# Five K-tile pairs in place of four by seven products in the two output stages of a two-layer float32 block

## The reference, cut to what matters

```
gate, up = split(h @ w_ffn_in)            # 2048 -> 2 x 5632
x = x + rms_norm((silu(gate) * up) @ w_ffn_out, g)   # first block; 5632 -> 2048
h = h + (silu(a) * b) @ ffn_w_out                    # second block, then a last rms_norm
```

## Time and profile before

| | us |
|---|---|
| median of 3 runs (lowest, highest) | 2390.25 (2389.15, 2392.04) |
| the profiled execution: its own time | 2391.39 |
| the profiled execution: its span | 2389.4 |
| TensorE busy in the span | 2369.1 (99%), 12027 instructions |
| VectorE busy | 1848.3 (77%), 2570 instructions |
| ScalarE busy | 1398.8 (59%), 1939 instructions |
| fo1, from its first unit to its last four | 1037.01 to 1262.57 |
| fo2, the same | 2147.10 to 2371.03 |

### The profile page before, as it was taken

How to read it: one execution, slowest core, us unless ns; L and a number is a source line. 1 busy time by engine, 2 the same in 40 slices (tenths; PEclk the granted TensorE clock), 3 DMA queues, 4 the chain that set the end, 5 groups by cost and what they waited for, 6 DMA issues and landing times.

```text
span 2389.4 us, 34793 instructions
## 1 busy us (share of the span) xinstructions
PE 2369.1 (99%) x12027; PEld 1977.8 (83%) x12027; DVE 1848.3 (77%) x2570; ACT 1398.8 (59%) x1939; POOL 195.2 (8%) x252
## 2 busy tenths in 40 slices
PE   9999999999999999999999999999999999999998
PEld 7888888887888888888887888998888888888887
DVE  5568878677899999987667535767799999997766
ACT  5665458656666666655445445655666666664444
POOL 1000000000111111200000000000121111111000
PEclk9999999999999999999999999999999999999999
DMA  7775554555889787866566775344788887867655
GB/s 233 244 217 177 165 152 165 167 186 176 273 205 248 207 230 227 222 199 208 196 212 196 219 231 168 126 140 133 241 229 243 212 246 207 234 176 242 217 179 176
DMA packets 249217, 485.23 MB, mean 203 GB/s; under 512 B 19770, under 2 KB 22074, under 8 KB 248592
## 3 DMA queue, kind: packets, MB, share of 16 engines
q1 hardware_dynamic: 216768, 410.51, 52.5%
q0 software_dynamic: 31760, 72.16, 14.9%
q10 hardware_dynamic: 576, 1.05, 0.1%
HBM read 474.21 MB, written 9.44 MB: 202 GB/s over the span
## 4 chain that ended last, share of the span: by engine, by line
PE 94%; DVE 3%; DMA 2%; ACT 1%; issue 1%; SPq 0%; ACTq 0%; DVEq 0%
PE g L1466 10%; PE g L1467 10%; PE g L1468 10%; PE g L362 6%; PE g L364 6%; PE g L363 6%; PE g L1973 4%; PE g L1975 4%; PE g L1974 4%; PE m L1294 3%; PE m L1295 3%; PE m L1293 3%; PE g L1294 2%; PE g L1295 2%; PE g L1293 2%; DMA raw<-in_w_ffn_out 1%
## 5 line engine op out<-in xcount | busy, mean ns | idle before, releaser
L350 DVE TENSOR_TENSOR wl<-raw,wh 128x1024 fp32r<-128x1024 f32 (+1 forms) x500 | 601.0, 1216 | 328.5 <-ACT wh L346 321.7
L346 ACT ACTIVATE wh<-raw 128x1024 fp32r<-128x1024 f32 (+1 forms) x499 | 519.1, 1052 | 468.1 <-PE g L364 128.8
L1466 PE MATMUL g<-wh,act_hi 128*128 128x512 f32 x640 | 250.5, 391 | 0.0
L1468 PE MATMUL g<-wh,act_lo 128*128 128x512 f32 x640 | 249.3, 390 | 0.0
L1467 PE MATMUL g<-wl,act_hi 128*128 128x512 f32 x640 | 249.3, 389 | 0.0
L1232 ACT ACTIVATE wh<-in_x 128x1024 fp32r<-128x1024 f32 (+1 forms) x160 | 152.7, 955 | 106.6 <-PE g L1468 69.5
L1466 PE MATMUL g<-wh,ht_hi 128*128 128x512 f32 x544 | 212.1, 390 | 0.3 <-DVE wl L350 0.3
L1467 PE MATMUL g<-wl,ht_hi 128*128 128x512 f32 x544 | 211.8, 389 | 0.0
L1468 PE MATMUL g<-wh,ht_lo 128*128 128x512 f32 x544 | 211.8, 389 | 0.0
L1394 DVE TENSOR_TENSOR wl<-raw,wh 128x1024 fp32r<-128x1024 f32 x160 | 195.5, 1222 | 13.1 <-ACT wh L1389 3.4
L362 PE MATMUL g<-wh,act_hi 128*128 128x512 f32 x512 | 203.3, 397 | 0.9 <-DVE wl L350 0.4
(11 more groups left out here) (546 smaller groups left out, 5116.8 us busy)
## 6 DMA issues: line engine op xcount, KB each, us to landing
raw<-in_w_in SPq DMA_DIRECT2D x111, 512.0 KB, 4.5
raw<-in_w_ffn_in SPq DMA_DIRECT2D x106, 512.0 KB, 4.8
raw<-in_ffn_w_in SPq DMA_DIRECT2D x106, 512.0 KB, 4.8
raw<-in_w_ffn_out SPq DMA_DIRECT2D x88, 512.0 KB, 5.3
raw<-in_ffn_w_out SPq DMA_DIRECT2D x88, 512.0 KB, 5.2
raw<-in_nsa_w_in SPq DMA_DIRECT2D x80, 512.0 KB, 4.3
raw<-in_w_out SPq DMA_DIRECT2D x32, 512.0 KB, 4.3
raw<-in_nsa_w_out SPq DMA_DIRECT2D x32, 512.0 KB, 4.9
```

What stands on the lines that cost most here:

```text
L346: nc.scalar.activation(wh[:, j % SLOTS, 0:n], raw[:, j % SLOTS, 0:n], ACT.Copy).then_inc(hi_done, 1)
L350: nc.vector.tensor_tensor(wl[:, j % SLOTS, 0:n], raw[:, j % SLOTS, 0:n], wh[:, j % SLOTS, 0:n].bitcast(F32), ALU.subtract).then_inc(lo_don ...
L1466: nc.tensor.matmul(dst, h, whk, start=(t in starts and k == 0), stop=False)
L1468: ins = nc.tensor.matmul(dst, l, whk, start=False, stop=(last and k == 1))
```

## The change: five pairs, new order, three rounds of sums

`FO_K` goes from 4 to 5. The order is written anew: blocks begin at positions 9, 18, 26, 35, 43 and 60, 69, 78, 87, 96 of 108. Sums of x come in three rounds, at positions 5, 14 and 28, the third for one pair alone. The first of the four sums now takes the place of the second row tile of the even K-tile in `ht_hi` and `ht_lo`, which blocks don't read, by an instruction of its own on ScalarE and VectorE; the other three stay in the buffers `fo_hi` and `fo_lo`, laid out anew.

```diff
-FO_K = 4
-FO_GAPS = ((10, 0), (5, 0), (1, 4), (1, 6), (1, 8)), ((6, 0), (6, 0), (4, 3), (1, 6), (1, 9))
-FO_SUMS_AT = (6, 15)
+FO_K = 5
+FO_GAPS = (((9, 0), (5, 0), (2, 2), (0, 5), (0, 4), (1, 6)),
+           ((6, 0), (5, 0), (5, 0), (0, 5), (0, 5), (1, 7)))
+FO_SUMS_AT = (5, 14, 28)
+FO_ROUNDS = (FO_K + 1) // 2
...
-        SUMMED = 3 * 2 + 2 + 3 * (FO_K // 2)
+        SUMMED = 3 * 2 + 2 + 3 * FO_ROUNDS
...
+        def in_round(r):
+            return min(2, FO_K - 2 * r)
...
                 if n - 2 in FO_SUMS_AT:
-                    b = FO_SUMS_AT.index(n - 2) + 1
-                    act_sums_hi(act, fo_sums[:, :, :, :], fo_hi[:, 2 * (b - 1):2 * b, :, :], summed_no(name, b) + 1)
+                    r = FO_SUMS_AT.index(n - 2)
+                    act.wait_ge(ff_summed, summed_no(name, r + 1) + 1)
+                    w = in_round(r)
+                    nc.scalar.activation(first_sums(ht_hi, 4 * r, w), fo_sums[:, 0:w, 0, :], ACT.Copy)
+                    act_sums_hi(act, fo_sums[:, 0:w, 1:4, :], fo_hi[r][:, :, :, :], summed_no(name, r + 1) + 1)
...
                 if n in FO_SUMS_AT:
-                    dve_sums_of_x(dve, ht_hi, ht_lo, 4 * FO_SUMS_AT.index(n), fo_whole, fo_sums)
+                    dve_sums_of_x(dve, ht_hi, ht_lo, 4 * FO_SUMS_AT.index(n), fo_whole, fo_sums, in_round(FO_SUMS_AT.index(n)))
                 if n - 2 in FO_SUMS_AT:
-                    b = FO_SUMS_AT.index(n - 2) + 1
-                    k = slice(2 * (b - 1), 2 * b)
-                    dve_sums_lo(dve, fo_sums[:, :, :, :], fo_hi[:, k, :, :], fo_lo[:, k, :, :], summed_no(name, b) + 1)
-                    dve.wait_ge(ff_summed, summed_no(name, b + 1))
+                    r = FO_SUMS_AT.index(n - 2)
+                    dve.wait_ge(ff_summed, summed_no(name, r + 1) + 2)
+                    w = in_round(r)
+                    nc.vector.tensor_tensor(first_sums(ht_lo, 4 * r, w), fo_sums[:, 0:w, 0, :], first_sums(ht_hi, 4 * r, w).bitcast(F32), ALU.subtract)
+                    dve_sums_lo(dve, fo_sums[:, 0:w, 1:4, :], fo_hi[r][:, :, :, :], fo_lo[r][:, :, :, :], summed_no(name, r + 1) + 1)
+                    dve.wait_ge(ff_summed, summed_no(name, r + 2))
```

More of the change, by code:

```diff
@@ L168, in build @@
         fo_sums = at("fo_sums", [P, 2, 4, P], o_al + 4096)
-        fo_hi = at("fo_hi", [P, FO_K, 4, P], o_ah, F32R)
-        fo_lo = at("fo_lo", [P, FO_K, 4, P], o_ah + 8192, F32R)
+        fo_hi = [at(f"fo_hi{r}", [P, 2 - r // 2, 3, P], o_ah + (0, 3072, 12288)[r], F32R) for r in range(FO_ROUNDS)]
+        fo_lo = [at(f"fo_lo{r}", [P, 2 - r // 2, 3, P], o_ah + (6144, 9216, 13824)[r], F32R) for r in range(FO_ROUNDS)]
         fo_kept = {"fo1": at("fo_kept1", [P, T, NB], o_ga + 4096), "fo2": at("fo_kept2", [P, T, NB], o_gb)}
@@ L1181, in pe_seven, with dve_sums_of_x @@
             product(3, 1, of_x(1, 1), g[:, 1, :], False, False).then_inc(unit_used, 1)
-        def dve_sums_of_x(dve, hi, lo, k0, whole, sums):
-            tiles = [b[:, k0:k0 + 4, :].bitcast(F32).rearrange("p (s k) (t n) -> p s k t n", s=2, t=T) for b in (hi, lo)]
+        def dve_sums_of_x(dve, hi, lo, k0, whole, sums, pairs=2):
+            tiles = [b[:, k0:k0 + 2 * pairs, :].bitcast(F32).rearrange("p (s k) (t n) -> p s k t n", s=pairs, t=T) for b in (hi, lo)]
+            whole, sums = whole[:, 0:pairs], sums[:, 0:pairs]
             link_d(dve, nc.vector.tensor_tensor(whole[:, :, :, :, :], tiles[0], tiles[1], ALU.add))
@@ L1200, in dve_sums_lo, with first_sums, fo_block_sums @@
             nc.vector.tensor_tensor(lo, sums, hi.bitcast(F32), ALU.subtract).then_inc(ff_summed, 1)
-        def first_sums(buf, r):
-            k0 = 2 * SEVEN_K + 4 * r
-            return buf[:, k0:k0 + 4:2, P:2 * P]
+        def first_sums(buf, k0, pairs=2):
+            return buf[:, k0:k0 + 2 * pairs:2, P:2 * P]
+        def in_round(r):
+            return min(2, FO_K - 2 * r)
+        def fo_block_sums(name, b):
+            return lambda n: ((fo_hi[b // 2][:, b % 2, n - 1, :], fo_lo[b // 2][:, b % 2, n - 1, :]) if n else
+                              (ht_hi[:, 2 * b, P:2 * P], ht_lo[:, 2 * b, P:2 * P]))
         def block_sums(b):
@@ L1510, in pe_out @@
                         pe.wait_ge(ff_summed, summed_no(name, 2 + b // 2))
-                    pe_seven(pe, cyc, n, ht_hi, ht_lo, 2 * b, lambda k: (fo_hi[:, b, k, :], fo_lo[:, b, k, :]),
+                    pe_seven(pe, cyc, n, ht_hi, ht_lo, 2 * b, fo_block_sums(name, b),
                              b == 0, b == FO_K - 1, s["pair0"][1] + c + 1)
@@ L1675, in opening @@
                 for r in range(2):
-                    ins = nc.scalar.activation(first_sums(act_hi, r), sums[r][:, :, 0, :], ACT.Copy)
+                    ins = nc.scalar.activation(first_sums(act_hi, 2 * SEVEN_K + 4 * r), sums[r][:, :, 0, :], ACT.Copy)
                 ins.then_inc(ff_summed, 1)
@@ L1718, in opening @@
                 for r in range(2):
-                    ins = nc.vector.tensor_tensor(first_sums(act_lo, r), sums[r][:, :, 0, :], first_sums(act_hi, r).bitcast(F32), ALU.subtract)
+                    ins = nc.vector.tensor_tensor(first_sums(act_lo, 2 * SEVEN_K + 4 * r), sums[r][:, :, 0, :], first_sums(act_hi, 2 * SEVEN_K + 4 * r).bitcast(F32), ALU.subtract)
                 ins.then_inc(ff_summed, 1)
```

## The result

The changed kernel takes 2396.9 us (median of 8 runs, 2394.33 to 2400.65) against 2390.28 (2389.15 to 2392.04) for the kernel before: ratio 1.0026, 95% interval 1.0017 to 1.0035. The forecast was 2391.7 with a range of 2388.0 to 2395.5. The sign was right, the time lies above the range, and the runs spread over 6.3 us where those of before spread over 2.9.

A forecast was written before the change was run, and what follows sets the result against it. TensorE, busy 99% of the span, was taken as the bound. The terms -2.72 + 1.4 + 0.9 + 0 + 0 + 1.93 = +1.5 us on the median 2390.25 gave 2391.7 us, with an 8-in-10 range of 2388.0 to 2395.5.

The forecast's parts named there:

- What bounds the kernel: Whole kernel: TensorE is busy 99% of the span, so only fewer products or TensorE waiting can move the time.
- Products: Output stages fo1 and fo2: 12 products fewer at 0.2267 us each, 2.72 us less on TensorE.
- the gain stands: Rival, chance 0.19: third round and fo2's close fit, -2.72, or -3.3 with the third block's wait gone: 2387.0 us.
- The third round: Third block of each output stage: VectorE's 1.9 us sums of x make TensorE wait 1.4 us in fo1, 0.9 in fo2.
- Second passes: Second pass of each output stage: five blocks start from a full ring of loaded weight slots; taken as 0.
- The end of fo1: Close of fo1: copying out the third column chunk comes a unit later; taken as 0, upper end 1.93 us.
- The end of fo2: Last four units of fo2: VectorE's closing steps delay their lo's, 1.93 us on the path, ends 0.8 and 3.0.
- The opening of fo1: Start of fo1: one wait grows about 0.3 us, the third block's goes; together 0, ends -1.6 and +1.4.
- the ring of loads becomes the bound: Rival, chance 0.14: two loads a step, one us longer, no longer fit in the first passes; 2396.6 us.
- From the profile to the median: Whole kernel: the profiled execution lies 1.14 us above the median, so 2392.9 us profiled became a forecast of 2391.7.

The follow-up runs named there:

- f1: The changed kernel with plain units' loads in both output stages bringing only 512 of 1024 columns: 2387.47 us, ratio 0.9986 against the kernel before.
- f2: The changed kernel with each block's three sums of weights in the output stages made for half their columns: 2391.34 us.
- h1: e3 plus a second own slot for the first weights of every other block, loaded inside the block before: 2390.0 us.
- e3: The changed kernel with the third round at position 32, not 28, and ten units, not eight, behind the last block of pass two: 2392.69 us.
- h2: e3 with the eight returning pieces of x issued two by two at the start of pass one's first four blocks: 2391.15 us.
- h4: The second slot of h1 and moved x of h2, with four blocks a pass and the kernel before's gaps and rounds: 2389.89 us.
- h3: e3 with both the second slot of h1 and the moved pieces of x of h2: 2387.81 us, ratio 0.9987 against the kernel before.
- f3: The changed kernel with the third round at 32 and pass two respaced: four units, two gaps of six, two of five: 2394.77 us.

## Why the prediction was wrong, step by step

**What bounds the kernel** was right, and so was the view that only TensorE's waits could take the gain away.

**Products**: right. TensorE has 12015 instructions, and f1, in which no output stage waits, is 3.5 us under the kernel before: the rival "the gain stands" put 3.3 on products and the third block's wait together.

**The third round**: right in place and size. It took 1.87 us (1099.70 to 1101.57; 1.9 forecast) between the lo's of the third and fourth quarter:

```profile
1098.57 1.22 DVE L352 TENSOR_TENSOR wl<-raw,wh 128x1024 fp32r<-128x1024 f32 x1
1099.70 0.69 DVE L1189 TENSOR_TENSOR fo_whole<-ht_hi,ht_lo 128x512 f32<-128x512 f32 x1
...
1101.28 0.29 DVE L1195 TENSOR_TENSOR fo_sums<-fo_whole,fo_sums 128x128 f32<-128x128 f32 x1
1101.49 2.35 DVE L352 TENSOR_TENSOR wl<-raw,wh 128x1024 fp32r<-128x1024 f32 x2
```

The third quarter lasted 2.44 us in place of 1.36 in fo1 and 2.43 in fo2: 1.08 and 1.07 against 1.4 and 0.9. The estimate by the Trainium skill (VectorE: DVE Perf Modes, The TRN2 errata) was 1.85.

**Second passes: this step failed.** "Five blocks five units apart start from a full ring; a step loses 0.7 or gains 0.2 by the intervals above. I take 0." In the profiled run TensorE waits at no block of a second pass, so the 0 itself came out there; what failed is the full ring that it rests on, and that the end of fo1 was to find. The steps of fo1 lost 2.5, 0.7, 0.2 and 0.7 of lead, and 4.28 us were gone at the fifth block. In fo2 the first step alone lost 3.8, and the others lay between 0.5 lost and 0.3 won. So the intervals were about right for a ring that is already low; that the first step takes most of a full ring's lead I left out. Two ends of opposite sign were averaged to 0, although the trace of before showed where the round comes from: the same two loads and sums in series. What that round hides was left out too: all loads wait while the sums are made, then come in one burst. f1, f2 and h1 show it by taking away bytes, sums and one load of the burst: 9.4, 5.6 and (against e3) 2.7 us.

**The end of fo1, taken as 0**, followed from it and paid 1.81, the largest miss of the sum inside the trace (its upper end was 1.93). VectorE's rows there, of the changed kernel, show the last two lo's of the last four starting only at 1266.10, behind the closing steps:

```profile
1258.79 0.68 DVE L1557 TENSOR_TENSOR fo_step<-fo_kept,m 128x512 f32<-128x512 f32 x1
1259.39 1.22 DVE L352 TENSOR_TENSOR wl<-raw,wh 128x1024 fp32r<-128x1024 f32 x1
1260.53 0.68 DVE L1561 TENSOR_TENSOR fo_kept<-fo_step,m 128x512 f32<-128x512 f32 x1
1261.24 1.23 DVE L1571 TENSOR_TENSOR g<-g,fo_kept 128x1024 f32<-128x1024 f32 x1
1262.51 1.23 DVE L352 TENSOR_TENSOR wl<-raw,wh 128x1024 fp32r<-128x1024 f32 x1
...
1264.96 1.22 DVE L513 TENSOR_TENSOR y_a<-g,g_b 128x1024 f32<-128x1024 f32 x1
1266.10 2.35 DVE L352 TENSOR_TENSOR wl<-raw,wh 128x1024 fp32r<-128x1024 f32 x2
```

**The end of fo2**: the size was right (1.93 forecast, 2.2 measured), the reason only in half. I laid VectorE's old rows under the new order, as if place alone decided. f1 has that place and no wait: with a full ring the lo's run far enough ahead to let the closing steps pass between (in fo2 the last lo, behind all of them, begins 2.35 us after TensorE began the last four units there, at 2370.15 against 2367.80, and 4.50 in the changed kernel, at 2377.91 against 2373.41).

**The opening of fo1**: taken as 0 net, about +1 measured (fo1 lost 0.86 + 1.36 - 1.08 = 1.1 us beyond the third round up to its last four units, most of it up to the third block's start). h2 gives it to the pieces of x.

**The rival "the ring of loads becomes the bound"** had 0.14 and 2396.6 us, 0.3 from the result. That the number came so near is luck: it priced 11.2 us of late loads in the first passes, less 6.3 of cover, and the trace has 1.5 us of idle at their units and blocks beside the third round's, nearly all in fo1. Its mechanism was the right one, its place only in half: I put it in the first passes, by the pieces of x (h2: 1.5 us), and gave the second passes nothing. What counted against it there, a full ring in the earlier trace rows, was read at the first block of the pass, before the denser blocks had drawn on it.

**From the profile to the median**: I carried the old distance over (1.14 above the median). The distance turned to 1.2 below: 2.3 of the 5.1 us by which the forecast missed. An explanation, not shown, is that a drained ring passes each late load on to TensorE. For it speaks the spread of f1 (1.6 us with half the bytes), and h4 (1.4), h3 (3.5) and e3 (5.6) fit; f3 (3.4, with an empty ring), h1 (6.4, with a fuller one) and h2 (6.1) don't. Why loads land later in some executions stays open.

## What to carry to other kernels

A full ring at the start of a stretch is a stock, not an income: work out what one round of it takes (loads as they land in their burst, and every step in series with them) against what the consumer needs. Do so for the first round by itself, since a full ring waits for its consumer: here that round left 1.75 and 0.50 of 4.28 us, and the later rounds gave nothing back. A piece on a side engine that seems to stand in the wrong place may cost nothing with the ring full, as in f1, so first ask why it was empty. By the times, a load moved into a pause of the DMA engines was worth more here than the new order of the same burst, and together with the moved pieces of x it gave the added blocks most of their gain back.

## What the runs showed of the hardware

Loads of 512 KB that go out together are later than I had counted: a median of 5.9 us in the burst of seven, 3.7 for those that h1 sends out in the pause. Halving 27 of 35 loads brought those to 3.1 and left the whole ones at 5.5. The pieces of x on POOL's queue lengthen SP's loads: with most of x moved away, the median in the opening of fo1 fell from 6.9 to 5.5 us (e3 and h2). And two programs with the same instructions on TensorE, VectorE and ScalarE spread by 1.6 us and by 6.3 (f1 and the changed kernel): where a change widens the spread, the loads are a first place to look, and one profiled execution then tells the time of the program less well than it did before.
